# Input chunks between value banks, a first normalisation on ScalarE, and reordered VectorE work in a fused mixer and expert kernel

## What is computed

```python
x = layer_norm(x, ln0_g, ln0_b)
mod = silu(c) @ ada_w + ada_b                  # six parts: sh1 sc1 g1 sh2 sc2 g2
h = x * (1 + sc1) + sh1
z = h @ w_in                                   # pooled part, recurrent part, gate
y = concat(pool_mixer(z), rglru_mixer(z)) @ w_out
x = layer_norm(ALPHA * x + g1 * y, ln1_g, ln1_b)
h = x * (1 + sc2) + sh2
q = normalise(h @ w_q)                         # 8 heads of 256, centred per head
e, g = two_stage_top_k(q @ k1, q @ k2)         # 16 experts a head and token
act = gelu(sum_d h[t, d] * u[e, d])
y = sum_k (g * act)[t, k] * v[e[t, k], :]
x = layer_norm(ALPHA * x + g2 * y, ln2_g, ln2_b)
```

## Time and profile before

| | |
|---|---|
| median of three runs | 1464.5 us (1463.25 to 1466.66) |
| profiled execution | 1464.51 us, span 1462.7 us |
| TensorE busy | 1420.2 us, 97% |
| VectorE busy | 1248.0 us, 85% |
| ScalarE busy | 583.1 us, 40% |
| GpSimd busy | 545.7 us, 37% |
| moved by DMA | 402.34 MB, mean 275 GB/s |

### The profile page before, as it was taken

How to read it: one execution, slowest core, us unless ns; L and a number is a source line. 1 busy time by engine, 2 the same in 40 slices (tenths; PEclk the granted TensorE clock), 3 DMA queues, 4 the chain that set the end, 5 groups by cost and what they waited for, 6 DMA issues and landing times.

```text
span 1462.7 us, 20651 instructions
## 1 busy us (share of the span) xinstructions
PE 1420.2 (97%) x7511; PEld 1233.0 (84%) x7511; DVE 1248.0 (85%) x2020; ACT 583.1 (40%) x689; POOL 545.7 (37%) x345
## 2 busy tenths in 40 slices
PE   7999999998999999999999999999999999999997
PEld 6775478898998989998888888888888888888885
DVE  8988969999999989756788888888898888888889
ACT  2561353332434878753233333333333333333331
POOL 0100225559564000000554545454555545554500
PEclk8999999999999999999999999999999999999999
DMA  9824440024645788999999999999999999999961
GB/s 383 314 115 173 150 185 1 1 78 148 223 168 186 241 263 267 273 321 355 326 361 364 355 369 356 372 355 366 362 364 376 364 358 362 380 355 370 355 228 57
DMA packets 158894, 402.34 MB, mean 275 GB/s; under 512 B 11344, under 2 KB 79056, under 8 KB 156144
## 3 DMA queue, kind: packets, MB, share of 16 engines
q1 hardware_dynamic: 120256, 262.17, 50.6%
q0 software_dynamic: 38288, 139.08, 25.2%
q10 hardware_dynamic: 288, 0.29, 0.1%
HBM read 359.56 MB, written 41.94 MB: 274 GB/s over the span
## 4 chain that ended last, share of the span: by engine, by line
PE 70%; DVE 9%; POOL 6%; issue 5%; DMA 4%; ACT 3%; SPq 2%; POOLq 0%; DVEq 0%; ACTq 0%
PE bank L973 21%; PE bank L971 21%; PE bank L972 21%; POOL u_lo L612 5%; DMA early_dram<-arena 2%; DMA u_raw<-ut_dram 2%; DVE arena L1303 1%; SPq L409 1%; PE bank L1056 1%; PE bank L1111 1%; PE bank L1115 1%; PE bank L1177 1%; PE bank L1179 1%; ACT arena L854 1%; DVE hsum L1494 1%
## 5 line engine op out<-in xcount | busy, mean ns | idle before, releaser
L971 PE MATMUL bank<-h_hi,u_hi 128*128 128x384 f32 (+1 forms) x1256 | 439.2, 350 | 8.8 <-POOL u_lo L612 6.2
L972 PE MATMUL bank<-h_lo,u_hi 128*128 128x384 f32 (+1 forms) x1256 | 433.0, 345 | 0.0
L973 PE MATMUL bank<-h_hi,u_lo 128*128 128x384 f32 (+1 forms) x1256 | 432.9, 345 | 0.0
L973 PE MATMUL bank<-v_hi,w_lo 128*128 128x512 f32 x744 | 295.0, 397 | 0.0
L972 PE MATMUL bank<-v_lo,w_hi 128*128 128x512 f32 x744 | 291.5, 392 | 0.0
L971 PE MATMUL bank<-v_hi,w_hi 128*128 128x512 f32 x744 | 290.1, 390 | 0.3 <-DVE w_lo L1712 0.3
L971 PEld LDWEIGHTS bank<-h_hi,u_hi 128*128 128x128 f32 x1256 | 235.8, 188 | 24.9 <-POOL u_lo L612 7.4
L1706 DVE TENSOR_TENSOR v_lo<-v_raw,v_hi 128x2048 fp32r<-128x2048 f32 x62 | 142.5, 2299 | 125.9 <-ACT v_hi L865 122.9
L972 PEld LDWEIGHTS bank<-h_lo,u_hi 128*128 128x128 f32 x1256 | 235.9, 188 | 11.7 <-issue 0.5
L973 PEld LDWEIGHTS bank<-h_hi,u_lo 128*128 128x128 f32 x1256 | 235.7, 188 | 9.4
L865 ACT ACTIVATE v_hi<-v_raw 128x2048 fp32r<-128x2048 f32 x62 | 118.9, 1918 | 310.3 <-PE bank L973 284.9
(11 more groups left out here) (243 smaller groups left out, 1823.3 us busy)
## 6 DMA issues: line engine op xcount, KB each, us to landing
u_raw<-ut_dram SPq DMA_DIRECT2D x128, 512.0 KB, 6.0
v_raw<-v_dram SPq DMA_DIRECT2D x64, 1024.0 KB, 6.4
gate_in<-gates_dram SPq DMA_DIRECT2D x64, 384.0 KB
wbuf<-ada_w_dram SPq DMA_DIRECT2D x9, 2048.0 KB, 13.1
early_dram<-arena SPq DMA_DIRECT2D x64, 192.0 KB, 1.9
gates_dram<-wbuf SPq DMA_DIRECT2D x3, 4096.0 KB, 16.5
w_raw<-early_dram SPq DMA_DIRECT2D x64, 192.0 KB
wbuf<-wq_dram SPq DMA_DIRECT2D x4, 2048.0 KB, 7.9
```

The lines of the kernel that those rows point to most:

```text
L971: pe.matmul(out, a_hi, b_hi, start=(k == 0), stop=False)
L972: pe.matmul(out, a_hi, b_lo, start=False, stop=False)
L973: return pe.matmul(out, a_lo, b_hi, start=False, stop=(k == n - 1))
```

## The change

1. The first normalisation moves from VectorE to ScalarE (an activation with scale 1/sd and bias -mean/sd). VectorE makes the bias (`mean_times_rstd`).
2. The decay terms move behind `low_weights_of(6)` on VectorE.
3. Spares: 12 to 8 at the start, none behind piece 1, 5 to 3 ahead of the second transposes.
4. Head sums are made head by head; the first half of the last residual comes ahead of head 2's, and head 3's comes behind the low input.
5. In the loop two chunks (6 matmuls) of the next input tile stand ahead of each of the first four value banks, and the waits for `w_lo` and `v_lo` behind the first two chunks instead of all eight.
6. VectorE's order in `prepare` changes: the gate block first, more picks ahead of `weigh`, `w_lo` ahead of `u_lo`.

```diff
-SPARE_FIRST, SPARE_ADA, SPARE_Z, SPARE_Q = 12, 2, 2, 5
+SPARE_FIRST, SPARE_Z, SPARE_Q = 8, 2, 3
...
                 root_of_variance(0, tb)
+            for tb in range(TB):
+                act.wait_ge(s_nmean, tb + 1)
+                act.activation(xt[:, tb, :], xt[:, tb, :], ACT.Identity, bias=nmean[:, tb:tb + 1],
+                               scale=rstd[:, tb:tb + 1]).then_inc(s_ln0, 1)
...
-                pe.wait_ge(s_ln, TB * (stage_of + 1))
+                pe.wait_ge(s_ln if stage_of else s_ln0, TB)
...
             upper_modulation(1)
-            spare(SPARE_ADA, 0)
             modulation(1)
...
-                expert_inputs(i, T_EARLY + c + 1, BANKS_SCATTER[(c + 1) % 2], i * RT + (T_EARLY + c))
-                pe.wait_ge(s_wlo, i * PER + (c + 1))
-                pe.wait_ge(s_vlo, i * PER + (c + 1))
-                for t in range(DENSE):
-                    for half in range(2):
-                        for j in range(2):
-                            w_of, v_of = pair_of(c % 2, j)
-                            mm = values(w_of, v_of, t, half, isinstance(i, int) and i + c + j == 0, False)
+                for o in range(OUTS):
+                    if 2 * o < KD:
+                        expert_inputs(i, T_EARLY + c + 1, BANKS_SCATTER[(c + 1) % 2], i * RT + (T_EARLY + c),
+                                      range(2 * o, 2 * o + 2))
+                    if o == 0:
+                        pe.wait_ge(s_wlo, i * PER + (c + 1))
+                        pe.wait_ge(s_vlo, i * PER + (c + 1))
+                    for j in range(2):
+                        w_of, v_of = pair_of(c % 2, j)
+                        mm = values(w_of, v_of, o // 2, o % 2, isinstance(i, int) and i + c + j == 0, False)
                 mm.then_inc(s_vmm, 1)
...
+            def mean_times_rstd(tb):
+                ve.wait_ge(s_sd, tb + 1)
+                link(ve.reciprocal(rstd[:, tb:tb + 1], sd[:, tb:tb + 1]))
+                ve.wait_ge(s_aggr, tb + 1)
+                ve.scalar_tensor_tensor(out=nmean[:, tb:tb + 1], in0=mv[:, tb, 0:1], scalar=-1.0,
+                                        in1=rstd[:, tb:tb + 1], op0=ALU.mult, op1=ALU.mult).then_inc(s_nmean, 1)
...
                 block_stats(tb)
-                if tb in (1, 2):
-                    decay_terms(tb - 1)
             for tb in range(TB):
-                normalise(0, tb)
+                mean_times_rstd(tb)
...
             low_weights_of(6)
+            decay_terms(0)
+            decay_terms(1)
             add_gate_row()
...
-            link(head_means(0))
-            scaled_means(0)
+            head_mean(0)
+            head_mean(1)
             residual(2)
-            link(head_means(1))
-            scaled_means(1)
+            last_residual(0)
+            head_mean(2)
             read_mod(24, 40, 10)
             scales(24, 32, "ln1_g", "ln1_b", scale2, bias2)
-            last_residual()
+            last_residual(1)
+            last_normalise()
             low_input(1, BANKS_X, scale2, bias2)
...
-            for j in range(2, 4):
-                link(head_means(j))
-                scaled_means(j)
+            for h in range(3, H):
+                head_mean(h)
...
                 n = PICKS_AT[c]
+                if 2 <= c < 10:
+                    add_late_gate_block(c - 2)
...
                     picks(1 if n else 0)
                     lo_v(c + 1)
-                    picks(1 if n > 1 else 0)
+                    picks(max(n - 2, 1) if n > 1 else 0)
                 weigh(c + 1)
-                picks(1 if n > 2 else 0)
+                picks((1 if n > 2 else 0) if c != AT_GELU * PER else n - 2)
+                lo_w(c + 1)
                 split_u(0, T_EARLY + c + 3)
-                picks(max(n - 3, 0))
-                lo_w(c + 1)
                 if c in (1, 2):
                     partial_modulation(11, range((c - 1) * KD // 2, c * KD // 2))
-                if 2 <= c < 10:
-                    add_late_gate_block(c - 2)
```

More of the change, by code:

```diff
@@ L322, in build @@
         s_vg = sem("last_values_gated")
+        s_nmean, s_ln0 = sem("mean_times_rstd"), sem("first_normalised")
         s_xs, s_xb, s_xl = sem("residual_stored"), sem("residual_back"), sem("last_residual_back")
@@ L956, in transposes @@
                 base = KD * stage_of
-                pe.wait_ge(s_ln, TB * (stage_of + 1))
+                pe.wait_ge(s_ln if stage_of else s_ln0, TB)
                 for k in chunks:
                     if stage_of and k == KD // 2:
-                        pe.wait_ge(s_ln, 2 * TB + 1)
+                        pe.wait_ge(s_ln, TB + 1)
                     if k >= len(banks):
@@ L1487, in _ @@
             affine(1)
-            def head_means(i):
-                wait_piece(ve, "wq", i)
-                for par in range(2):
-                    w = piece("wq", i)[:, :, par * DK:(par + 1) * DK]
-                    last = ve.tensor_reduce(hsum[:, i * 2 + par, :], w, AX.X, ALU.add)
-                return last
-            def scaled_means(i):
-                for h in (2 * i, 2 * i + 1):
-                    ve.tensor_scalar(hmean[:, h, :], hsum[:, h, :], -1.0 / DK, None, ALU.mult).then_inc(s_hmean, 1)
@@ L1501, in last_residual, with head_mean @@
-            def last_residual():
+            def head_mean(h):
+                wait_piece(ve, "wq", h // 2)
+                w = piece("wq", h // 2)[:, :, h % 2 * DK:(h % 2 + 1) * DK]
+                link(ve.tensor_reduce(hsum[:, h, :], w, AX.X, ALU.add))
+                ve.tensor_scalar(hmean[:, h, :], hsum[:, h, :], -1.0 / DK, None, ALU.mult).then_inc(s_hmean, 1)
+            def last_residual(half):
                 tb = TB - 1
                 ve.wait_ge(s_x0, tb + 1)
-                for half in range(2):
-                    n = 2 * tb + half
-                    piece_x = xt[:, tb, half * 512:(half + 1) * 512]
-                    ve.wait_ge(s_ymm, n + 1)
-                    ve.tensor_tensor(y_gated[:, n % 4, :], bank[n % Y_BANKS][:, :],
-                                     row_gate[:, half * 512:(half + 1) * 512], ALU.mult).then_inc(s_yres, 1)
-                    ve.wait_ge(s_yres, n + 1)
-                    link(ve.scalar_tensor_tensor(out=piece_x, in0=piece_x, scalar=ALPHA,
-                                                 in1=y_gated[:, n % 4, :], op0=ALU.mult, op1=ALU.add))
-                    last = ve.bn_stats(st[:, tb, half, :], piece_x)
-                link(last)
@@ new lines, in last_residual @@
+                n = 2 * tb + half
+                piece_x = xt[:, tb, half * 512:(half + 1) * 512]
+                ve.wait_ge(s_ymm, n + 1)
+                ve.tensor_tensor(y_gated[:, n % 4, :], bank[n % Y_BANKS][:, :],
+                                 row_gate[:, half * 512:(half + 1) * 512], ALU.mult).then_inc(s_yres, 1)
+                ve.wait_ge(s_yres, n + 1)
+                link(ve.scalar_tensor_tensor(out=piece_x, in0=piece_x, scalar=ALPHA,
+                                             in1=y_gated[:, n % 4, :], op0=ALU.mult, op1=ALU.add))
@@ L1516, in last_residual, with last_normalise @@
+                link(ve.bn_stats(st[:, tb, half, :], piece_x))
+            def last_normalise():
+                tb = TB - 1
                 ve.bn_aggr(mv[:, tb, :], st[:, tb, :, :]).then_inc(s_aggr, 1)
```

## The result

The kernel after takes 1471.89 us (median of seven runs, 1469.68 to 1476.92), the kernel before 1463.41 beside it: a ratio of 1.0054, 95% interval 1.004 to 1.0068. It is slower by half a per cent, where I had forecast 1461.1 us and at most 1465.6. The profiled execution took 1471.89 us, with a span of 1470.1 against 1462.7: 7.4 us to be found.

A forecast was written before the change was run, and what follows sets the result against it. It took the chain of waits as the bound, TensorE holding 70% of it and VectorE 9%. Its terms summed to -3.4 us, from the median 1464.5 to 1461.1 us, range 1457.8 to 1465.6.

The forecast's parts named there:

- Place A: First 42 us, up to the first projection: VectorE freed earlier, column sums sooner, -3.6 us; late clock rise, +0.3.
- rival 2: Clock: TensorE at 1.2 GHz into the projection (Place A) or queries (Place B), 1.6 us each, 1464.3 us; chance 0.17.
- Place B: 174 to 186 us, mixer output to second transposes: residual's second half sooner, -1.7 us; head 3's sum delays queries, +0.45.
- Decay terms: Moved behind the convolution: their 3.0 us covered by VectorE's wait before 88.59 and TensorE's projections, 0; 1.5 us without cover.
- Pair 0: Loop start: 18 input matmuls held behind the w_lo wait, +3.13 us, pair 3's 2.31 us gate-block wait gone; net +0.35.
- Changes of kind: Loop, 57 pairs: three more switches each direction between input and value matmuls, 0 to 1.7 us, taken as +0.5.
- Slack of the loop: Steady loop: w_lo ready 1.4 us before TensorE asks for it, 5.9 before the change; cost 0 while that holds.
- Rival 1: Loop slack breaks through VectorE's pick and w_lo or picked rows: with 0.15 us, +8.6, 1469.7 us; chance 0.1.
- End: After the last pair: VectorE leaves about 1.0 us later, partly offset by waits it had before; +0.3 us.

The follow-up runs named there:

- decay experiment: The kernel after with the decay terms one place further back, behind the add of the gate row: 1470.14 us, ratio 1.0032 to the kernel before.
- fourteen executions: The profiled executions of the kernel before, the kernel after and the twelve follow-up kernels, one each.
- pair 0 experiment: The kernel after, but pair 0 alone takes all its input matmuls first, other pairs staying interleaved: 1466.95 us, ratio 1.0013 to the kernel before.
- loop order alone: The kernel before with only TensorE's interleaved pair of the kernel after: 1615.28 us, ratio 1.1014 to the kernel before.
- inputs whole: The kernel after with all 24 input matmuls of a pair ahead of its values: 1461.59 us, ratio 0.9969; later kernels kept this order.

## Why the prediction was wrong

My sum was -3.4 us, the profiled executions differ by +7.4. By its own steps:

- **Place A, -3.6 + 0.3.** Measured -2.85 at the first transposes and -1.2 at the end of the sixth tile. VectorE was free at 12.3 (predicted 12.9), the column sums ended at 35.80 (35.0): the weights landed 0.7 us later than my lag allowed. The clock took 1.6 us at the sixth tile and not 0.3; 1.6 was the upper bound I gave. Of the total it is hardly a part, as the wait for the gate row hid it (decay experiment). I had taken the 0.3 because spares "still end about 1 us ahead, as before"; by the fourteen executions, spares of before or of after, half clock there is the common case. What this step sized from one execution of before was a draw. Of rival 2, place A came true and place B didn't; with all the spares the half clock at A came as well. The Trainium skill ("TensorE: Matmul & The Clock Gate", section "What's actually happening") says that the point of the rise varies by 500 ns, and also that one kernel can show it at quite different matmuls from run to run. The traces agree that it varies and disagree with the 500 ns: here the stretch at half clock behind the first projection matmul was absent in four executions and about 3 us or more in ten.
- **Decay terms, 0 (bound 1.5). This step failed in kind.** I covered 3.0 us of VectorE with a wait it has at 88.59, and with "TensorE's projections". But the instruction right behind the terms is the add of the gate row, and TensorE waits for that one at 77 us. The wait at 88.59 stands behind it and could pay nothing back. It cost +3.6 us from 77.08 to 87.50: 2.35 from the last projection matmul on, and 1.25 because the gate matmuls ran slower; with the terms one place further back, 3.7 came back.
- **Place B, -1.7 + 0.45.** Measured -1.66 at the transposes; the queries' wait is 0.41 us longer. Right, and in the place that the rows named.
- **Pair 0, +0.35.** Measured +2.3. The 18 held inputs were 3.1 us as computed and the gate block's 2.31 came back, which makes 0.8: the 0.35 came of setting a computed time (695.0) beside a measured one (694.65). Missing was the clock: the idle 3.4 us were followed by half clock from 660.8 to 664.3, about 1.5 us lost. As the pair 0 experiment shows, the early wait by itself cost 4.7 us.
- **Changes of kind, +0.5 (bounds 0 to 1.7). The term that was mis-sized most.** Measured +4.7 (717.63 - 712.90) over 57 pairs: 0.027 us for each added change a direction, 0.08 a pair. I had read one change in the earlier trace rows, the gap ahead of the first value, as 0.18 against a step of 0.174. The price doesn't lie in that gap. It lies in the second to fourth six inputs of a pair, 1.06 to 1.07 us each against 1.04 in the whole order, too little for a reading of one gap with steps of 0.01 us.
- **Slack of the loop, 0.** Right but for 0.16 us in one pair: 1.4 us predicted, 1.4 measured. Rival 1 gave the time best (1469.7, +8.6 us) and for another reason: it had a slack broken in every pair, and that didn't come. Its nearness is luck. The kernel with the loop order alone shows what it would have been.
- **End, +0.3.** The span gained 0.8 us from the inputs behind the loop on. Over the executions with inputs whole that tail varies from 53.4 to 55.0 us; I make nothing of it.

Together: -1.2 + 3.6 - 1.25 + 0.05 + 2.3 + 4.7 - 0.8 = +7.4 us, the 0.05 being what moved between the queries and pair 0. By size, the loop's changes of kind put the forecast on the wrong side, and with pair 0 and the decay terms they make over 10 us of loss where I had 0.85.

The parts of the change fall into three: interleaving (a loss of about 10 us by the medians, 1471.9 to 1461.6, and 9.7 in the trace; by the ratios 12; and it needs part 6), the decay terms (a gain of 2.9 at the start, given back behind the sixth tile), and head sums (-1.3 in its place). The spares and the moved normalisation made no difference that these runs can tell (1460.52 and 1460.77 us beside 1460.72).

## What to carry to other kernels

When work is moved on an engine, look for the first thing that another engine awaits behind its new place; a wait of the same engine further on covers nothing of it. Where a small price is repeated in a loop that one engine fills entirely, read it over many repetitions (the length of 50 iterations, or one kernel with the pattern doubled), never from one gap. And a wait put in front of a dense stretch can cost more than its length, since slower matmuls can follow it.

## What the hardware showed

- Changes between blocks of input matmuls (128x384, operands h and u) and value matmuls (128x512, v and w) cost 0.027 us for an added change to and fro from 1 over 2 to 4 (12.48, 12.507, 12.56 us a pair) and less up to 8 (12.61 where no wait is near). The time stands in the input blocks that follow six values (1.06 to 1.07 us for six inputs); that behind 18 values takes 1.04, as in a whole block. Changes of output bank alone, 12 for 6 a pair, cost nothing (12.48).
- TensorE's busy share and granted clock showed nothing of it: 100.00 us busy in 100, clock 1.00, in both kernels.
- Stretches at 1.2 GHz came and went between executions of kernels in which TensorE had the same instructions there. Behind the wait for the gate row in five kernels with the decay terms ahead, the gate matmuls took 8.8 us in four (behind 2.1 to 3.75 us of wait) and 7.1 in one (behind 2.2). At the start of the first projection ten of fourteen executions had such a stretch and four had none. Near 300 to 350 us the mean clock was 0.93 over 25 us in some executions and 1.00 in others. Each such stretch takes 1 to 1.8 us of TensorE's work, as much as several parts of this change, but not always of the total: that at A was hidden behind the gate row.
